# Router of a two-layer diffusion backbone: 16-bit gate products in two parts, interleaved with the key searches and the query products

## What is computed

```python
q = (x @ wq).reshape(t, PEER_HEADS, 2, PEER_HALF)                  # 8 heads, two halves of 128
sc = jnp.einsum('thpc,hpnc->thpn', q, keys)                        # 128 keys for each half
s_top, i_top = lax.top_k(sc, PEER_TOPK)                            # 16 best of each half
cand = (s_top[:, :, 0, :, None] + s_top[:, :, 1, None, :])         # their sums
cs, ci = lax.top_k(cand, PEER_TOPK)                                # 16 best sums
i1 = take_along_axis(i_top[:, :, 0], ci // PEER_TOPK); i2 = take_along_axis(i_top[:, :, 1], ci % PEER_TOPK)
g = softmax(cs)                                                    # the gates
out = sum over the picked experts of  gelu(u[i1 * 128 + i2] . x) * g * v[i1 * 128 + i2]
```

## Time and profile before

| | |
|---|---|
| time, median of 3 runs | 3227.99 us (3226.13 to 3228.69) |
| time of the profiled execution | 3230.49 us, span 3228.7 us |
| PE busy | 3113.9 us (96%) |
| DVE busy | 2859.2 us (89%) |
| POOL busy | 1953.4 us (61%) |
| ACT busy | 1111.0 us (34%) |
| 2 MB chunk of query or "ada" weights, from issue to landing | 7.5 or 7.6 us (32 and 19 of them) |
| half a tile's gates to DRAM, 4 MB, from issue to landing | 11.6 us (12 of them) |

### The profile page before, as it was taken

How to read it: one execution, slowest core, us unless ns; L and a number is a source line. 1 busy time by engine, 2 the same in 40 slices (tenths; PEclk the granted TensorE clock), 3 DMA queues, 4 the chain that set the end, 5 groups by cost and what they waited for, 6 DMA issues and landing times.

```text
span 3228.7 us, 50364 instructions
## 1 busy us (share of the span) xinstructions
PE 3113.9 (96%) x15946; PEld 2600.8 (81%) x15946; DVE 2859.2 (89%) x5542; ACT 1111.0 (34%) x1693; POOL 1953.4 (61%) x1483
## 2 busy tenths in 40 slices
PE   7998999989999999999998999979999999999998
PEld 6857566679999999999996467669999999999997
DVE  3474599899999999999998599999999999999998
ACT  3332333333333333333333233333333333333333
POOL 1000166667777887777662057767778776777774
PEclk9999999989999999999998999989999999999998
DMA  5230456689999999999996344589999999999996
GB/s 239 79 135 29 157 221 251 257 341 409 408 406 405 403 402 389 407 408 406 402 410 265 131 189 202 228 313 406 409 406 401 404 403 386 399 399 407 402 404 231
DMA packets 248396, 1044.93 MB, mean 324 GB/s; under 512 B 23024, under 2 KB 72944, under 8 KB 205808
## 3 DMA queue, kind: packets, MB, share of 16 engines
q0 software_dynamic: 147456, 536.94, 42.0%
q1 hardware_dynamic: 100848, 506.86, 39.8%
HBM read 990.49 MB, written 53.22 MB: 323 GB/s over the span
## 4 chain that ended last, share of the span: by engine, by line
PE 82%; DVE 7%; issue 5%; DMA 4%; POOL 1%; ACT 1%; DVEq 0%; SPq 0%; POOLq 0%; ACTq 0%
PE bankA L1601 10%; PE bankA L1603 10%; PE bankA L1602 10%; PE bankA L1555 7%; PE bankD L1614 6%; PE bankD L1615 6%; PE bankD L1613 6%; PE bankD L1523 5%; PE bankA L1615 3%; PE bankA L1614 3%; PE bankA L1613 3%; DMA hT<-in_v,idxc 1%; DVE wch L1377 1%; DMA wch<-in_wq 1%; PE bankD L1803 1%
## 5 line engine op out<-in xcount | busy, mean ns | idle before, releaser
L1601 PE MATMUL bankA<-hh,uh 128*128 128x384 f32 x2048 | 688.6, 336 | 24.7 <-DVE ul L1361 24.7
L1603 PE MATMUL bankA<-hh,ul 128*128 128x384 f32 x2048 | 688.7, 336 | 0.0
L1602 PE MATMUL bankA<-hl,uh 128*128 128x384 f32 x2048 | 687.3, 336 | 0.0
L685 POOL DMA_INDIRECT hT<-in_v,idxc x320 | 461.4, 1442 | 179.6 <-issue 66.8
L685 POOL DMA_INDIRECT hT<-in_u,idxc x320 | 468.3, 1463 | 159.3 <-issue 74.2
L811 ACT ACTIVATE wt<-bankA 128x384 f32<-128x384 f32 x256 | 126.0, 492 | 1021.1 <-PE bankA L1603 838.0
L1601 PEld LDWEIGHTS bankA<-hh,uh 128*128 128x128 f32 x2048 | 385.8, 188 | 36.1 <-issue 26.3
L1377 DVE SCALAR_TENSOR_TENSOR wch<-hT,a,wch 128x1024 f32<-128x1024 f32 x320 | 399.5, 1278 | 11.3 <-DMA hT<-in_v,idxc 7.6
L1614 PE MATMUL bankD<-vl,wh 128*128 128x512 f32 x1024 | 399.8, 390 | 0.0
L1615 PE MATMUL bankD<-vh,wl 128*128 128x512 f32 x1024 | 399.3, 390 | 0.0
L1613 PE MATMUL bankD<-vh,wh 128*128 128x512 f32 x1024 | 398.3, 389 | 0.0
(11 more groups left out here) (246 smaller groups left out, 5611.3 us busy)
## 6 DMA issues: line engine op xcount, KB each, us to landing
uraw<-in_uT SPq DMA_DIRECT2D x128, 1024.0 KB
vraw<-in_vP SPq DMA_DIRECT2D x128, 1024.0 KB
wch<-in_wq SPq DMA_DIRECT2D x32, 2048.0 KB, 7.5
gates_scratch<-gbuf SPq DMA_DIRECT2D x12, 4096.0 KB, 11.6
wch<-gates_scratch SPq DMA_DIRECT2D x64, 768.0 KB
wch<-in_ada SPq DMA_DIRECT2D x19, 2048.0 KB, 7.6
wch<-in_qkv SPq DMA_DIRECT2D x3, 2048.0 KB, 23.8
adap<-in_ada SPq DMA_DIRECT2D x3, 2048.0 KB, 17.1
```

What stands on the lines that cost most here:

```text
L685: pool.indirect_dma_start(out=row_buf[slot], out_offset=None, in_=table.rearrange("l e d -> (l e) d"), in_offset=bass.IndirectOffsetOnAxis ...
L1601: pe.matmul(abank[c], hi, hh[:, k, :], start=k == 0, stop=False)
L1602: pe.matmul(abank[c], hi, hl[:, k, :], start=False, stop=False)
L1603: last = pe.matmul(abank[c], lo, hh[:, k, :], start=False, stop=k == K - 1)
```

## The change

It changes only how the router does its work; the dense part and the gathers stay.

1. **16-bit slots of 8 tokens.** HOT is 8 and SLOTS 3, so there are 16 slots per tile and 48 per layer. The one-hots (`hot`) are fp16: 2,048 values per partition and slot. The numbers that they are compared with are written twice next to each other (`num16`), and the row of 0..127 (`iotap`) lies in PSUM in fp16. A gate is split into a high and a low fp16 part after scaling by 2^14. GpSimd makes the high part of a slot (`high_part`, one instruction of 1,024 values), ScalarE the low part of the first four tokens and VectorE that of the other four (`low_part`, one tensor_scalar of 128 values per token, with the token's low gate as a per-partition scalar).
2. **TensorE** takes two fp16 matmuls of 128 x 128 per token (high, then low) instead of one in fp32; ScalarE's copy to `gbuf` scales back.
3. **Interleaving.** VectorE's one-hots and low parts stand between the instructions of the searches of units 3 to 8: `between()` is called after each search instruction, every 7th call issues a slot's one-hots, and the slot's low part comes 4 search instructions later. TensorE and ScalarE have the gates of one slot after every 2 query matmuls, 4 slots behind VectorE. GpSimd adds up the key numbers of unit u - 1 in one run at the start of unit u and then makes the high parts of that unit's 8 slots.
4. The second candidate buffer is gone (match_replace works in place), softmax sums move into the search, stores of gates are issued per half tile, and the "ada" chunks stand behind the units 4 to 9.

```diff
-HOT = 4
-SLOTS = 4
+HOT = 8
+SLOTS = 3
+NSLOT = P // HOT
+ALL_SLOTS = DT * NSLOT
+FIRST_HOT = 3
+PER_UNIT = 8
+LAG = 4
+AHEAD = 2
+ACT_RESTS = 4
+PACE = 7
...
+    for u in range(-1, UNITS):
+        for r in range(PER_UNIT):
+            c, part = 2 * u + 2 + r // 4, r % 4
+            if c < CHUNKS:
+                o.append(("wq", L, c // 4, chunk_at(c // 4, c % 4), part))
+                if c and part < 2:
+                    o.append((("turn", "score")[part], L, c - 1))
...
+            q = PER_UNIT * (u - FIRST_HOT) + r
+            if 0 <= q - LAG < ALL_SLOTS:
+                g = q - LAG
+                o.append(("gates", L, g))
...
-                hot = sb("hot", [P, SLOTS, 2, HOT, P], where=rt)
+                hot = sb("hot", [P, SLOTS, HOT, 2, P], F16, where=rt)
+                parts = sb("parts", [P, SLOTS, 2, HOT, P], F16, where=rt)
...
-        iotap = bankD[0][:, 512:512 + P]
+        iotap = bankD[0][:, 512:512 + P // 2]
...
+                def high_part(g):
+
+                    G, t = L * ALL_SLOTS + g, g // NSLOT
+                    t0 = g % NSLOT * HOT
+                    pool.wait_ge(hot_ready, G + 1)
+                    pool.tensor_tensor(
+                        parts[:, G % SLOTS, 0, :, :], hot[:, G % SLOTS, :, 0, :],
+                        high[:, t % 2, t0:t0 + HOT].unsqueeze(2).to_broadcast([P, HOT, P]), ALU.mult).then_inc(high_ready, 1)
...
+                for u in range(UNITS):
+                    for r in range(PER_UNIT):
+                        if u and r == 0:
+                            weigh(u - 1, 0)
+                            weigh(u - 1, 1)
+                            fold_eight(u - 1)
+                            fold_rest(u - 1)
+                        g = PER_UNIT * (u - FIRST_HOT) + r
+                        if 0 <= g < ALL_SLOTS:
+                            high_part(g)
...
+                            i, r = divmod(n, PACE)
+                            if r == 4 and i < PER_UNIT:
+                                one_hots(PER_UNIT * (unit - FIRST_HOT) + i)
+                            if r == 1 and 1 <= i <= PER_UNIT:
+                                low_part(PER_UNIT * (unit - FIRST_HOT) + i - 1)
...
+                def one_hots(g):
+
+                    G = L * ALL_SLOTS + g
...
+                    if G >= SLOTS:
+                        v.wait_ge(g_full, 2 * (G - SLOTS + 1))
+                    twos = lambda x: x.rearrange("p (i two) -> p i two", two=2)
+                    v.tensor_tensor(
+                        hot[:, G % SLOTS, :, :, :].rearrange("p t c (i two) -> p (t c) i two", two=2),
+                        num16[:, t0:t0 + HOT, :, :].rearrange("p t c two -> p (t c) two").unsqueeze(2).to_broadcast(
+                            [P, 2 * HOT, P // 2, 2]),
+                        twos(iotap.bitcast(F16)).unsqueeze(1).to_broadcast([P, 2 * HOT, P // 2, 2]), ALU.is_equal
+                    ).then_inc(hot_ready, 1)
+
+                def low_part(g):
+
+                    G, t = L * ALL_SLOTS + g, g // NSLOT
+                    v.wait_ge(hot_ready, G + 1)
+                    for i in range(ACT_RESTS, HOT):
+                        n = g % NSLOT * HOT + i
+                        last = v.tensor_scalar(parts[:, G % SLOTS, 1, i, :], hot[:, G % SLOTS, i, 0, :],
+                                               low[:, t % 2, n:n + 1], None, ALU.mult)
+                    last.then_inc(rest_dve, 1)
...
-                    if 1 <= t <= DT:
-                        one_hots(t - 1)
...
+                pe.wait_ge(high_ready, G + 1)
+                pe.wait_ge(rest_act, G + 1)
+                pe.wait_ge(rest_dve, G + 1)
```

More of the change, by code:

```diff
@@ L172, in next_ada @@
     def next_ada():
+        if len(done) >= len(late):
+            return []
         unit = late[len(done)]
@@ L236, in build @@
                 held = None
-            elif unit[0] == "gates":
-                behind.append((len(chunks) + 1, unit[2]))
+            elif unit[0] == "store":
+                behind.append((len(chunks), unit[2:4]))
         LAST_LOAD[len(chunks) - 1] = L
-        for n, t in behind:
-            STORES.setdefault(min(n, len(chunks) - 1), []).append((L, t))
+        for n, (t, half) in behind:
+            STORES.setdefault(min(n, len(chunks) - 1), []).append((L, t, half))
     CN = {c[0]: n for n, c in enumerate(chunks)}
@@ L1228, in search @@
                         o += ni * w
+                        between()
                     summed = mark(last)
@@ L1234, in search @@
                     v.wait_ge(step, summed)
-                    most = [mark(v.max(csv[:, h, 0:8], cand[:, h, 0:NCAND])) for h in range(HALF)]
+                    most, rest = [0] * HALF, [0] * HALF
+                    for h in range(HALF):
+                        most[h] = mark(v.max(csv[:, h, 0:8], cand[:, h, 0:NCAND]))
+                        between()
                     for h in range(HALF):
@@ L1255, in search @@
                         last.then_inc(gexp_in, 1)
-                    before = t - 1 if t and not p else None
-                    if before is not None:
-                        v.wait_ge(gexp_out, L * TILES + t)
-                        added = mark(v.tensor_reduce(gsum, heads(gt[:, before % 2, :]), AX.X, ALU.add))
                     v.wait_ge(step, chosen)
@@ new lines, in gate_numbers, with gate_rests @@
+                    v.tensor_copy(num16[:, :, :, :],
+                                  bankD[0][:, 0:2 * P].rearrange("p (j t) -> p t j", j=2).unsqueeze(3).to_broadcast([P, P, 2, 2]))
+                    sums.append(mark(v.tensor_scalar(high[:, t % 2, :], bankD[0][:, 2 * P:3 * P], GSCALE, None, ALU.mult)))
+                def gate_rests(t):
+                    v.wait_ge(step, sums[-1])
+                    v.scalar_tensor_tensor(out=low[:, t % 2, :], in0=bankD[0][:, 2 * P:3 * P], scalar=GSCALE,
+                                           in1=high[:, t % 2, :], op0=ALU.mult, op1=ALU.subtract).then_inc(pickT_ready, 1)
@@ L1539, in route @@
             def route(L):
-                waiting = None
                 for name in route_order(L):
                     kind = name[0]
-                    if name in R:
+                    if kind in ("ada", "adat"):
                         n = R[name]
                         bank = ring[L][n % 2]
-                        if n >= 2:
+                        pe.wait_ge(r_free, n - 1)
+                    if kind == "wq":
+                        whole, t, part = name[0:4], name[2], name[4]
+                        n = R[whole]
+                        bank = ring[L][n % 2]
+                        if part == 0 and n >= 2:
@@ L1548, in route @@
                             pe.wait_ge(r_free, n - 1)
-                    if kind == "wq":
-                        w = chunk(name)
-                        t = name[2]
-                        for k in range(K):
+                        if part == 0:
+                            rows = chunk(whole)
+                        for k in range(2 * part, 2 * part + 2):
                             if t == 0 and name[3] == 0:
                                 pe.wait_ge(h_ready, (1 + 2 * L) * K + k + 1)
-                            last = pe.matmul(bank, hT[:, k, t * P:(t + 1) * P], w[:, k, :], start=k == 0, stop=k == K - 1)
-                            if waiting is not None and k == 0:
-                                turn(waiting)
-                            if waiting is not None and k == 2:
-                                score(waiting)
-                        last.then_inc(r_full, 1)
-                        waiting = (L * TILES + t) * 4 + place_of(t, name[3])
-                        continue
@@ L1563, in route @@
-                    if kind == "picks":
+                            last = pe.matmul(bank, hT[:, k, t * P:(t + 1) * P], rows[:, k, :], start=k == 0, stop=k == K - 1)
+                        if part == 3:
+                            last.then_inc(r_full, 1)
+                    elif kind == "turn":
+                        turn(L * CHUNKS + name[2])
+                    elif kind == "score":
+                        score(L * CHUNKS + name[2])
+                    elif kind == "picks":
                         picks(L, name[2])
-                        continue
@@ L1566, in route @@
-                    if kind == "ada":
+                    elif kind == "gates":
+                        gates(L, name[2])
+                    elif kind == "ada":
                         w = chunk(name)
```

286 lines of the change are left out of this document (147 added, 139 removed).

## The result

The changed kernel takes **3305.25 us** (median of 4 runs, 3302.89 to 3307.67), the kernel before 3227.06 us on the same chip (3225.85 to 3228.69). The ratio is 1.0242, with a 95% interval of 1.0224 to 1.026: 78 us slower, where 37 were forecast.

The account below looks back on a forecast made before the run. TensorE and VectorE were both taken as full in the routers. Units of 30.5 + 9.6 = 40.1 us against 36.05 and 37.97 before added 37 us, giving 3265 us, range 3170 to 3320 us.

Parts of the forecast that it names:

- The unit of 40.1 us: Router units 3 to 8: VectorE's work of 30.5 us plus 9.6 us of waits for GpSimd per unit.
- One-hots at the double rate: VectorE's 16-bit one-hots: 2,048 values cost what 1,024 did, 1.13 us each, 9.1 us per unit.
- Rival B: One-hots at one value at a time because an operand is in PSUM: 48.5 us units, 3366 us; chance 0.09.
- The port excludes a tensor_scalar of fp16: VectorE's low parts and GpSimd instructions exclude each other (the port): one works, the other waits for the whole instruction.
- Rival A: VectorE's low parts don't wait for GpSimd: 31.5 us units, 3179 us, down to 3160; chance 0.25.
- I take 1.2 us each: Low parts' wait for GpSimd per slot, 8 slots: 9.6 us per unit, bounds 1.0 to 1.5 us.
- Fit into the slack of TensorE at 40 us: Layer 0's "ada" chunks, about 3 us of product and a 7.5 us load, were costed at nothing.
- The tail in layer 1: Unit 9 and what follows until the first `scan`: the last 30.6 us, left about as they are.
- Rival C: GpSimd keeps its turn or TensorE's clock falls to the lower level: 46 us units, 3336 us; chance 0.06.
- The ring of three slots adds some: Slot 3's comparison waits for slot 0's product, its high part starting after 8.6 us; included in 1.2 us per slot.
- the two stretches: Start of unit 3 to the first `scan` in each layer's router: 246.9 us in layer 1, 258.4 in layer 0 before.
- the forecast's + 37: Six units of 240.6 us per layer: + 24.3 us in layer 1 and + 12.8 us in layer 0, together.

Follow-up runs that it names:

- e1: The changed kernel with VectorE's four low parts per slot merged into one tensor_tensor, both operands in SBUF; 3271.92 us.
- e2: The changed kernel with VectorE's four low parts as one tensor_tensor reading its gates from a copy in PSUM; 3229.39 us.
- e4: The changed kernel with all eight low parts of a slot on ScalarE and none on VectorE; 3218.69 us.
- e6: The changed kernel with GpSimd's key-number run split up, ahead of a unit's first four high parts; 3321.76 us.
- e5: The changed kernel with only layer 0's "ada" chunks placed elsewhere and passed through the other weight buffer while shared query chunks stay; 3299.58 us.
- e8: e2 with the "ada" chunk placement and loading of e5; 3210.53 us.
- e12: e4 with "ada" chunks loaded as in e5 but placed singly until three in unit 9, and gate stores queued one load later; 3176.19 us.

## Why the prediction was right in its direction and wrong in its size

- **The unit of 40.1 us** became 42.4 us in layer 1. VectorE's time there, each instruction counted from its start to the next one's (1921.41 to 2175.63), splits into 101.6 us of low parts (192), 53.8 of one-hots (48) and 98.8 of the rest. The forecast's six units were 89.4, 54.6 and 96.6.
- **One-hots at the double rate**: right, 1.199 us for 2,048 values. Rival B fell with it. The Trainium skill's tier table ("VectorE: DVE Perf Modes", The perf-mode tier table), by which any PSUM operand makes tensor_tensor 1x, doesn't hold for this form.
- **The port excludes a tensor_scalar of fp16**: right. All 114 long low parts of the changed kernel ended within 54 ns of a GpSimd instruction's end; e1 against e2 shows the exclusion for a tensor_tensor with both inputs in SBUF. Rival A fell, and its condition was then made: without the waits e2 has units of 33.8 us in layer 1 and e4 of 33.1, near the 31.5 that it gave. Most of the difference in e2 is VectorE's wait for the ring of three slots, 13.4 us in six units. The rule in "SBUF — State Buffer" (Who interferes with whom) of the Trainium skill agrees with the trace: the later of the two blocks for the whole instruction (1.04 us instead of 0.24 beside the high part in the fence above).
- **The step that failed is "I take 1.2 us each"**, the wait per slot. It measured (101.6 / 48) - 0.65 = 1.47 us, near the upper bound of 1.5: the mechanism held, and this term of the sum was too small. The step let the four low parts of a slot wait once and then keep the port. The first wait was sized well, 1.08 us on average. But in the first two slots of every unit GpSimd slips in between the low parts, and the run waits again (behind 2.12 and 1.14 us in the fence above). These further waits are 0.38 us per slot, 18.4 us per layer, and were not in the sum. The low parts take 12 us more than forecast in layer 1 (101.6 against 89.4) and as much in layer 0 (101.6 too), 24 of the 38 us below. e6, with three such slots in a unit for two, lost 16 us more.
- **"Fit into the slack of TensorE at 40 us"** failed as well. The "ada" chunks were costed at product and load one by one, but not as users of a ring of two buffers. In layer 0 that is 5.4 us in the units (259.6 against 254.2) and most of 3.6 us at the tail, which the last "ada" load (15.2 us of wait) set. e5 gives the tail's 3 us back and in the units only 1; the cost there shows in e2 against e8, which have no waits for the port (232.3 and 209.1 us of units), and not by an edit to the changed kernel.
- **The tail in layer 1**, taken as 30.6 us, was 31.2.
- Rival C had TensorE's clock fall. It did fall, 0.97 to 0.84 of the upper level in layer 1, while the engine stood idle between slots. It cost nothing that shows in layer 1, since VectorE was busy 284.4 of the 285.5 us.
- **"The ring of three slots adds some"**: in layer 1 of the changed kernel it added nothing (no idle time stands before `L1412`), the waits for the port covered it. It shows once they are gone, with 13.4 us in e2's six units of layer 1 and 27.1 in e12's.
- Together: 2 x 13.6 us in units, 5.4 for layer 0's chunks, 4.2 at the tails, and 1.6 before unit 3, that is 38 us by which the two stretches of the profiled execution exceed the forecast's + 37. That the median missed 3265 by nearly as much, 40 us, is in part chance: the rest of the profiled execution was 3.6 us shorter, and the profiled executions lie 5.8 us closer together than the medians.

## What to carry to other kernels

When VectorE work is put beside GpSimd work, count the moments at which the port is handed over and not only the busy sums. Each short VectorE instruction of an excluded kind (here a tensor_scalar in SBUF, or a tensor_tensor with both inputs there) can wait for a whole long one on GpSimd, and several in a row can wait several times. One merged instruction takes the repeated waits away, another engine or an operand in PSUM takes all of them (here 4.4, 9.3 and 8.5 us of a unit's 42.4). Under a bound that is removed look for the next one at once: here the ring of two weight buffers and a store that stood ahead of a ready load in SyncE's queue held most of layer 0's units at 38 to 43 us, and mending both was worth some 42 us (e4_act_all to e12_one_each, on different chips) beside the 87 of the first bound. Under these lies a third, the ring of three slots behind GpSimd's run.

## What the runs showed of the hardware

- Four tensor_scalars in a row don't hold the port: GpSimd's waiting instruction got in after the first one, 0.23 us, and its next one ahead of the fourth. In a profile such a wait is part of the instruction's busy time; what gave it away is a mean of 608 ns over a median of 242.
- A tensor_tensor with one operand in PSUM and the other in SBUF ran beside GpSimd's two-operand instruction with neither stretched (668 and 1,935 ns). The one-hots, with 16-bit values in all operands and one of them in PSUM, went at 0.59 ns per value (2,048 in 1.199 us). The merged low parts took 1.3 ns per value with the gates in PSUM and in SBUF alike (512 values in 0.668 and at least 0.669 us); their gates are fp32 in both places (`aval` and `bankD`), and are broadcast over 128 values, and no run here tells which of the two costs the double rate.
- With both operands in SBUF the exclusion costs both sides: GpSimd's high part went from 1,935 to 2,124 ns on average in e1.
